# A mixture-of-experts stage with a fourth size class, its own PSUM banks for the down product, and weight loads half as large

## What is computed

```python
def expert(args):
    xe, e = args
    hu = xe @ w_up[e] + b_up[e]                       # (slots, 1024) @ (1024, 2048)
    gate = jnp.minimum(hu[:, :D_FF], SWIGLU_LIMIT)
    lin = jnp.clip(hu[:, D_FF:], -SWIGLU_LIMIT, SWIGLU_LIMIT)
    glu = gate * jax.nn.sigmoid(SWIGLU_ALPHA * gate)
    return ((lin + 1.0) * glu) @ w_down[e] + b_down[e]  # (slots, 1024) @ (1024, 1024)
```

## Time and profile before

| | before |
|---|---|
| median of the runs shown | 1485.96 us |
| span of the profiled execution | 1487.5 us |
| TensorE busy | 1238.6 us (83%) |
| VectorE busy | 402.2 us (27%) |
| ScalarE busy | 226.0 us (15%) |
| mean rate of the DMA over the span | 315 GB/s |
| mean granted TensorE clock | 0.934 of full speed |

### The profile page before, as it was taken

How to read it: one execution, slowest core, us unless ns; L and a number is a source line. 1 busy time by engine, 2 the same in 40 slices (tenths; PEclk the granted TensorE clock), 3 DMA queues, 4 the chain that set the end, 5 groups by cost and what they waited for, 6 DMA issues and landing times.

```text
span 1487.5 us, 21559 instructions
## 1 busy us (share of the span) xinstructions
PE 1238.6 (83%) x8297; PEld 615.4 (41%) x8306; DVE 402.2 (27%) x838; ACT 226.0 (15%) x376; POOL 94.1 (6%) x154
## 2 busy tenths in 40 slices
PE   3899898679649989989878998879967789897796
PEld 2554455545434444434324443434323333343243
DVE  0144113661471322112211211221212221232116
ACT  1211223001220110111111011110111111111111
POOL 0010002331330000000000000000000000000002
PEclk7799999888869999999999999999999999999998
DMA  9676537138214699899999789999899999999992
GB/s 311 243 217 188 179 113 214 49 114 244 113 57 173 270 418 382 338 382 417 419 418 418 315 338 385 417 418 419 330 418 416 419 419 419 415 418 419 418 416 109
DMA packets 116009, 467.94 MB, mean 315 GB/s; under 512 B 6978, under 2 KB 26118, under 8 KB 82953
## 3 DMA queue, kind: packets, MB, share of 16 engines
q1 hardware_dynamic: 100466, 455.61, 78.4%
q10 hardware_dynamic: 14966, 9.78, 2.2%
q0 software_dynamic: 544, 2.10, 0.6%
HBM read 461.31 MB, written 6.16 MB: 314 GB/s over the span
## 4 chain that ended last, share of the span: by engine, by line
PE 56%; DMA 33%; DVE 5%; ACT 2%; issue 2%; SPq 1%; POOL 0%; ACTq 0%; POOLq 0%; PEldq 0%; DVEq 0%
DMA mem<-in_w_up 31%; PE psum L780 19%; PE psum L811 8%; PE psum L513 6%; PE psum L822 3%; PE psum L757 3%; PE psum L498 3%; PE psum L697 2%; PE psum L517 1%; DMA mem<-in_w_mod 1%; PE psum L424 1%; PE psum L641 1%; ACT mem L1132 1%; PE psum L825 1%; DVE mem L1625 1%
## 5 line engine op out<-in xcount | busy, mean ns | idle before, releaser
L780 PE MATMUL psum<-mem 128*32 128x512 f32 (+2 forms) x2048 | 421.3, 630 | 126.8 <-DMA mem<-in_w_up 74.9
L780 PEld LDWEIGHTS psum<-mem 128*32 128x32 f32 (+2 forms) x2048 | 135.9, 133 | 406.8 <-issue 277.0
L811 PE MATMUL psum<-mem 128*32 128x512 f32 (+2 forms) x1024 | 204.8, 594 | 1.7 <-DMA mem<-in_w_down 1.7
L1718 DVE TENSOR_SCALAR mem<-psum 128x256 f32<-128x256 f32 (+2 forms) x32 | 20.0, 626 | 647.5 <-PE psum L785 647.5
L811 PEld LDWEIGHTS psum<-mem 128*32 128x32 f32 (+2 forms) x1024 | 102.9, 130 | 79.8 <-issue 50.6
L1737 DVE TENSOR_TENSOR mem<-mem,psum 128x1024 f32<-128x1024 f32 (+1 forms) x96 | 100.0, 1045 | 88.9 <-PE psum L822 71.2
L822 PE MATMUL psum<-mem 128*128 128x512 f32 x264 | 121.4, 602 | 1.2 <-ACT mem L1132 1.2
L1116 ACT ACTIVATE mem<-mem 128x256 f32<-128x256 f32 (+2 forms) x32 | 18.5, 579 | 483.3 <-DVE mem L1718 483.3
L757 PEld LDWEIGHTS psum<-mem 128*128 128x128 bf16 x2376 | 80.5, 99 | 21.4 <-issue 20.4
L513 PE MATMUL psum<-mem 128*128 128x512 f32 x192 | 86.3, 606 | 1.6 <-PE psum L424 1.6
L757 PE MATMUL psum<-mem 128*128 128x32 bf16 (+2 forms) x2376 | 83.9, 192 | 2.1 <-DVE mem L1694 2.1
(11 more groups left out here) (244 smaller groups left out, 918.5 us busy)
## 6 DMA issues: line engine op xcount, KB each, us to landing
mem<-in_w_up SPq DMA_DIRECT2D x128, 2048.0 KB, 23.5
mem<-in_w_down SPq DMA_DIRECT2D x64, 2048.0 KB, 19.7
mem<-in_w_mod SPq DMA_DIRECT2D x12, 2048.0 KB, 15.7
mem<-in_w_in SPq DMA_DIRECT2D x8, 2048.0 KB, 12.8
mem<-in_w_out SPq DMA_DIRECT2D x2, 2048.0 KB, 10.6
mem<-in_state_ret SPq DMA_DIRECT2D x4, 512.0 KB, 6.3
mem<-in_state_mlstm_c SPq DMA_DIRECT2D x4, 512.0 KB, 7.2
out_ret_s<-mem ACTq DMA_DIRECT2D x4, 512.0 KB, 3.2
```

The source lines that it names most:

```text
L780: last = pe.matmul(out, xg[:, 2 * c + j, 0:slots], moving, start=(c == 0 and j == 0), stop=False)
L811: last[c] = pe.matmul(psum[slots * q:slots * q + slots, 2 + u, :], actT[:, j, slots * q:slots * q + slots], at((4 + c) * SLOT, 4, D)[:, pi ...
```

## The change

1. A fourth size class of 96 slots. Experts with 65 to 96 tokens (0, 3 and 11) leave the class of 128. `up` for them does three groups of 32 slots (banks 0, 1, 2) times four quarters of the output columns, each matmul with 32 stationary columns in one column group: 96 matmuls of 512 columns, 192 records. `down` runs untiled with 96 stationary columns. The activations need 6 transposes in place of 8, their copy out is split in two by order, and VectorE's clips have 768 columns.
2. Twelve loads of 1 MB an expert, eight of w_up (one contraction piece each) and four of w_down, each with its own arrival and release semaphore. `down` waits for each w_down piece at its first use and gives each free at its last.
3. The down result goes to banks 6 and 7; the scatters go to banks 2 and 3, then 4 and 5, then 3; the placement transposes to bank 2. The wait for `y_copied` moves from ahead of `up` to ahead of the first scatter, where two waits for VectorE's clips are added (the scatter overwrites banks 2 and 3). The waits for `G_ready` and `added` move ahead of `up`.

```diff
-SIZES = (32, 64, 128)
+SIZES = (32, 64, 96, 128)
@@ by_size
+            with eng.If(count <= SIZES[1]):
+                with eng.If(count <= SIZES[0]):
+                    f(SIZES[0])
+                with eng.Else():
+                    f(SIZES[1])
+                eng.nop()
             with eng.Else():
-                with eng.If(count <= SIZES[1]):
-                    f(SIZES[1])
+                with eng.If(count <= SIZES[2]):
+                    f(SIZES[2])
                 with eng.Else():
-                    f(SIZES[2])
+                    f(SIZES[3])
+                eng.nop()
@@ SyncE
+            def expert_piece(e, c):
+                if c < UP:
+                    src = a["w_up"][0][e, 128 * c:128 * c + 128, :]
+                    dst = piece_slot(c, 2 * D)
                 else:
+                    src = a["w_down"][0][e, 256 * (c - UP):256 * (c - UP) + 256, :].rearrange("(j p) n -> p j n", p=128)
+                    dst = piece_slot(c, 2, D)
+                sp.dma_start(dst, src).then_inc(piece_in[c], 16)
             with sp.Fori(1, NE) as e:
-                for c in range(6):
-                    sp.wait_ge(used[c], e + USES[c])
-                    expert_chunk(e, c)
+                for c in range(PIECES):
+                    sp.wait_ge(piece_done[c], e)
+                    expert_piece(e, c)
@@ TensorE, up
-                if slots == 32:
+                if slots in (32, 96):
                     w = weights.rearrange("p (l n) -> p l n", l=2)
-                    return [(psum[32 * q:32 * q + 32, 0, :], w[:, :, 256 * q:256 * q + 256]) for q in range(4)]
+                    return [(psum[32 * q:32 * q + 32, g, :], slice(32 * g, 32 * g + 32), w[:, :, 256 * q:256 * q + 256])
+                            for g in range(slots // 32) for q in range(4)]
...
+                for c in range(UP):
+                    pe.wait_ge(piece_in[c], 16 * (it + 1))
+                    for out, cols, moving in up_products(slots, piece_slot(c, 2 * D)):
+                        last = pe.matmul(out, xg[:, c, cols], moving, start=(c == 0), stop=False)
+                    last.then_inc(piece_done[c], 1)
@@ TensorE, down
-                tiles = 128 // slots
+                tiles = 1 if slots == 96 else 128 // slots
...
-                for c in (4, 5):
-                    pe.wait_ge(loaded[c], 16 * (it + USES[c] + 1))
+                            if last[c] is None:
+                                pe.wait_ge(piece_in[UP + c], 16 * (it + 1))
...
-                last[0].then_inc(used[4], 1)
-                last[1].then_inc(used[5], 1)
+                for c in range(DOWN):
+                    last[c].then_inc(piece_done[UP + c], 1)
@@ TensorE, expert
                 pe.wait_ge(S("xg_ready"), ig + 1)
-                pe.wait_ge(S("y_copied"), it + 1)
+                pe.wait_ge(S("G_ready"), it + 1)
+                pe.wait_ge(S("added"), 3 * it + 1)
                 by_size(pe, count, lambda slots: up(it, slots))
                 gather(ig + 1, count_next)
-                pe.wait_ge(S("G_ready"), it + 1)
-                pe.wait_ge(S("added"), 3 * it + 1)
+                pe.wait_ge(S("y_copied"), it + 1)
+                pe.wait_ge(S("gate_ready"), it + 1)
+                pe.wait_ge(S("lin_clipped"), it + 1)
                 scatter(it, 0)
...
                 scatter(it, 2)
-                pe.wait_ge(S("added"), 3 * it + 3)
                 by_size(pe, count, lambda slots: down(it, slots))
@@ ScalarE, expert
+                    if slots == 96:
+                        by_piece = actT.rearrange("p j s -> p (j s)")[:, 0:n] \
+                            .rearrange("p (q h g s) -> p h g q s", q=4, h=2, g=3)
+                        by_turn = flat(0, n).rearrange("p (g h q s) -> p h g q s", g=3, h=2, q=4)
+                        act.copy(by_piece[:, 0], by_turn[:, 0])
+                        act.copy(by_piece[:, 1], by_turn[:, 1]).then_inc(S("actT_ready"), 1)
+                        return
...
-                act.copy(yd.rearrange("p u n -> p (u n)"), flat(2, D)).then_inc(S("y_copied"), 1)
+                act.copy(yd.rearrange("p u n -> p (u n)"), flat(6, D)).then_inc(S("y_copied"), 1)
```

More of the change, by code:

```diff
@@ L258, in build, with piece_slot @@
         used = [S(f"slot{c}_used") for c in range(6)]
+        UP, DOWN = 8, 4
+        PIECES = UP + DOWN
+        piece_in = [S(f"piece{c}_in") for c in range(PIECES)]
+        piece_done = [S(f"piece{c}_done") for c in range(PIECES)]
+        def piece_slot(c, *shape):
+            return at(c * SLOT // 2, *shape)
         def by_size(eng, count, f):
             if count is None:
-                f(SIZES[2])
+                f(SIZES[3])
                 return
-            with eng.If(count <= SIZES[0]):
-                f(SIZES[0])
+            with eng.If(count <= SIZES[1]):
[4 more added lines that the diff above has]
+                eng.nop()
             with eng.Else():
-                with eng.If(count <= SIZES[1]):
-                    f(SIZES[1])
+                with eng.If(count <= SIZES[2]):
+                    f(SIZES[2])
                 with eng.Else():
-                    f(SIZES[2])
+                    f(SIZES[3])
+                eng.nop()
         def flat(bank0, n):
@@ L390, in _ @@
                     with sp.Fori(0, NE) as e:
-                        for c in range(6):
-                            sp.wait_ge(used[c], r * NE + e + USES[c])
-                            expert_chunk(e, c)
+                        for c in range(PIECES):
+                            sp.wait_ge(piece_done[c], r * NE + e)
+                            expert_piece(e, c)
             with sp.Else():
@@ L763, in up_products @@
             def up_products(slots, weights):
[L766 removed]
+                if slots in (32, 96):
                     w = weights.rearrange("p (l n) -> p l n", l=2)
[L768 removed]
+                    return [(psum[32 * q:32 * q + 32, g, :], slice(32 * g, 32 * g + 32), w[:, :, 256 * q:256 * q + 256])
+                            for g in range(slots // 32) for q in range(4)]
                 if slots == 64:
[L770 removed]
+                    return [(psum[64 * q:64 * q + 64, lin, :], slice(0, 64),
+                             weights[:, D * lin + 512 * q:D * lin + 512 * q + 512])
                             for lin in range(2) for q in range(2)]
[L772 removed]
+                return [(psum[:, b, :], slice(0, 128), weights[:, 512 * b:512 * b + 512]) for b in range(4)]
             def up(it, slots):
[L775 to L782 removed]
+                for c in range(UP):
[3 more added lines that the diff above has]
+                    last.then_inc(piece_done[c], 1)
                 pe.wait_ge(S("bsel_ready"), it + 1)
[L784 to L785 removed]
+                for out, cols, moving in up_products(slots, bparts[:, 0:2 * D]):
+                    last = pe.matmul(out, bsel[:, cols], moving, start=False, stop=True)
                 last.then_inc(S("up_done"), 1)
@@ L809, in down @@
                             piece = q * pieces + j
[L810 to L813, removed]
+                            c = piece // 2
+                            if slots == 96:
+                                turned = actT.rearrange("p j s -> p (j s)")[:, 0:8 * slots] \
+                                    .rearrange("p (j s) -> p j s", j=KD)[:, piece, :]
+                            else:
+                                turned = actT[:, j, slots * q:slots * q + slots]
+                            if last[c] is None:
+                                pe.wait_ge(piece_in[UP + c], 16 * (it + 1))
+                            last[c] = pe.matmul(psum[slots * q:slots * q + slots, 6 + u, :], turned,
+                                                piece_slot(UP + c, 2, D)[:, piece % 2, 512 * u:512 * u + 512],
                                                 start=(j == 0 and q > 0), stop=(j == pieces - 1))
-                last[0].then_inc(used[4], 1)
-                last[1].then_inc(used[5], 1)
+                for c in range(DOWN):
+                    last[c].then_inc(piece_done[UP + c], 1)
             def scatter(it, t):
[L820 to L826, removed]
+                for u in range(2):
+                    out = psum[:, 2 + 2 * t + u, :] if t < 2 else psum[64 * u:64 * u + 64, 3, :]
+                    last = pe.matmul(out, G[:, tok(t)], yd[:, u, :], start=True, stop=True)
                 last.then_inc(S("scattered"), 1)
@@ L1128, in expert @@
                 act.wait_ge(S("scattered"), 3 * it + 3)
-                act.copy(G, psum[:, 7, 0:NTOK]).then_inc(S("G_ready"), 1)
-                act.wait_ge(used[4], it + 1)
-                act.wait_ge(used[5], it + 1)
-                act.copy(yd.rearrange("p u n -> p (u n)"), flat(2, D)).then_inc(S("y_copied"), 1)
+                act.copy(G, psum[:, 2, 0:NTOK]).then_inc(S("G_ready"), 1)
+                for c in range(UP, PIECES):
+                    act.wait_ge(piece_done[c], it + 1)
```

(7 more changed lines are left out.)

26 lines of the change are left out of this document (10 added, 16 removed).

## The result

The changed kernel takes 1949.56 us (four runs, 1946.22 to 1952.41) against 1485.39 us before (four runs, the three above and one of 1484.83): ratio 1.311, 95% interval 1.308 to 1.314. It is 31% slower, and nowhere near the 1440 us of the forecast.

The account below looks back on a forecast made before the run. Weight loads at 418 GB/s set the pace, with about 61 us of idle DMA around large experts. Gains 9.7 + 37.7 + 2.8 less 2.7 for boundaries make 47.5; 1487.5 - 47.5 = 1440.0 us, range 1431 to 1462.

Parts of the forecast that it names:

- The size class of 96: Large experts on TensorE: `up` 21.3 us in place of 29.4, 9.0 to `down`, `down` 13.75; sum 44.1 us.
- The banks: Between `down` and the next expert: the result's copy leaves the path, 1.64 us before, 0.2 taken for the branch.
- Rival 4: TensorE's loop: waits, deeper branches and the new arm's code add 3 us or more per expert; 1475 to 1490, chance 0.04.
- the walk: Large experts 0, 3, 11 and 17 followed in turn: gains of 9.7 and 37.7 us, 3 us idle left.
- The rival that 96 slots don't pack: Class-96 `up` stays 29.4 us, 8.1 longer three times, 21 us in all; time 1461, chance 0.11.
- Expert 0: Start of the loop: `up` ends at 475.0, `down` runs 484.0 to 497.7, expert 1's weights land earlier; gain 9.7 us.
- Behind expert 3: DMA after this large expert: w_down pieces come free before the queue needs them, idle 0 in place of 13.5 us.
- the 0.015 us: Cost taken for each of six added load boundaries per expert, 2.7 us over 30 experts.
- the 0.09 us of one window: Worst microsecond near a load boundary, 381 of 418; upper bound per added boundary, in a rival 16.6 us, time 1454, chance 0.14.
- Expert 30's last w_up piece: Sign near the end of the loop: it lands near 1371 us, before 1416.

Follow-up runs that it names:

- the kernel with the short loop: The changed kernel with the gather in two arms (64 and 128 slots) in place of four, all else kept: 1442.11 us, ratio 0.970.

## Why the prediction was wrong, point by point

**The step that failed** is the one that priced the new arm: "The size class of 96". It counted the 192 records that run and what they replace, and took the arm's code for free; the branch got 0.2 us under "The banks". The part that lies in no row of the trace before is the length of the code. It shows there only as an absence: 23 packets of the instruction queue, none in the loop. Rival 4 had the right kind of cause ("the new arm's code") with "3 us or more" an expert in it, a chance of 0.04 and a time of 1475 to 1490. The measured size is 16.4 us an expert: 1949.56 - 1442.11 = 507.5 over 31.

**What would have shown it beforehand.** The built program of before could be counted: 1,187 instructions in the loop, and 657 more by the change. No trace of before shows how many fit, so the 1,844 would have been a reason for a wide range and no more; a run of the kernel before with arms that nobody takes shows it without the change (1,743 fast, 1,791 slow).

**The rest of the walk mostly held**, as the kernel with the short loop shows, in which only the gather's arms differ from the change. Its chain (start, length, what):

```profile
451.18 20.81 PE psum L800 x192
...
498.50 7.05 PE psum L800 x64
...
523.88 1.06 PE psum L800 x8
...
538.98 20.81 PE psum L800 x192
...
568.82 13.73 PE psum L835 x32
582.55 13.88 PE psum L800 x64
...
1280.34 1.94 PE psum L800 x8
...
1340.58 1.87 PE psum L800 x8
```

- Class 96: `up` 20.81 us against 21.3 forecast, `down` 13.73 against 13.75; 538.98 to 582.55 is 43.6 against 44.1. The rival that 96 slots don't pack was wrong: 192 records took 0.108 us each, against 0.111 in class 32, so three groups of 32 keep all four column groups at work.
- Expert 0: expert 1 begins at 498.50 (497.9 forecast), but in part by luck. The stage began 0.9 us earlier. The forecast's end of `up`, 475.0 = 452.06 + 21.3 + 1.6, has 1.6 us for a low clock at its start (before, the first 2 MB took 9.0 us against 29.43 / 4 = 7.4 later, at a mean granted clock of 0.81). No run shows such a loss for 96 slots: here the granted clock was 1.00 from 451 to 461 us, and `up` took 20.81 us. What took that back is the way from the end of `up` (471.99) to `down` (484.76): 12.8 us in place of 9.0, with 1.9 us of "issue" inside the gather and slower scatters.
- Expert 2's last piece of w_up landed at 523.8, while 501.5 + 20.1 = 521.6 was forecast, so less of the idle time around expert 0 went than the 9.7 us. Expert 2 waited for that piece, where the forecast had it at TensorE's pace; so expert 3 begins at 538.98 (536.6 forecast). Expert 4 begins at 582.55, against 536.6 + 44.1 + 0.2 = 580.9.
- The banks: between the end of `down` (568.82 + 13.73 = 582.55) and the next `up` (582.55) nothing is left of 1.64 us.
- Idle time of the DMA, by windows of the same kernel:

```profile
454.50:501.00 46.50, 44.62 (x327) 17.28 (x323) 8.35 (x13) 4.25 (x7) 0.29 (x1) 0.96 0.67 255
501.00:590.00 89.00, 87.92 (x729) 36.14 (x723) 20.90 (x39) 13.83 (x20) 0.88 (x3) 1.00 1.02 418
590.00:650.00 60.00, 58.43 (x493) 24.99 (x490) 16.23 (x30) 9.66 (x14) 0.59 (x2) 1.00 1.02 418
...
830.00:920.00 90.00, 85.18 (x647) 34.59 (x644) 21.37 (x41) 13.56 (x20) 0.88 (x3) 0.97 1.00 409
920.00:1040.00 120.00, 111.84 (x758) 48.52 (x759) 27.54 (x51) 17.33 (x24) 1.18 (x4) 0.97 1.01 412
1040.00:1370.00 330.00, 285.16 (x2105) 106.80 (x2097) 72.97 (x143) 45.65 (x66) 3.23 (x11) 0.93 1.02 418
```

  Behind expert 3 nothing is idle (13.5 us before). Two windows below 418 are left, 90 x (1 - 409/418) = 1.9 and 120 x (1 - 412/418) = 1.7, together 3.6 against 3 forecast. The last window lies at 418 with twelve loads an expert, and two experts take 1340.58 - 1280.34 = 60.24 us, 30.12 each against 30.11 before. So no cost of a boundary shows: the 0.015 us (2.7 us in all) was not needed, and the 0.09 us of one window was no cost of a boundary.
- Expert 30's last w_up piece ended its wait at 1370.7, where about 1371 was forecast. That is luck in part: the start around expert 0 was 2.2 us worse, and the stretch behind it 2.2 us better, as the boundaries cost nothing.
- The release of w_down: the sections before the prediction say that both w_down slots come free only at the end of `down`. With 128 slots the first comes free halfway, as the prediction takes it and the earlier trace rows show (an issue from 497.99, in a `down` that ended at 504.7). With 32 slots all pieces come free at the end in both kernels.
- Sum: 1487.5 - 1439.4 = 48.1 us between the spans, against 47.5.
- The parts: without the class of 96 a gain of 29.6 us was measured against 1486.85 (20 expected); the class adds 15.2 to that, the smaller pieces 15.1. They don't add up to shares of their own, since each takes idle time that another would have taken.

So the forecast's own mechanism came to within 2 us once the loop was short, with two errors of 2.2 us that cancelled, and the answer was off by 510 us by a resource that it had not looked at.

## What to carry to other kernels

Before adding an arm to a branch in a loop, count the loop's instructions on the engine as built, dead arms included, and look at the instruction queue's packets inside the loop: none means that it fits, and that says nothing about how near it is to not fitting (here 25 packets in all at 1,743 instructions, 305 at 1,791). If idle time called "issue" appears at places without a wait, at changing spots of the same group of matmuls (here behind 53 and behind 35 of 72), look at that queue first. A branch arm that saves little (here the gather for 32 slots in place of 64, 0.3 us: 1.90 against 2.21 us before) can be dropped to pay for one that saves much.

## What was not expected of the hardware

- A loop of about 1,743 instructions on TensorE ran without fetches (25 packets of q8 in all), one of 1,791 with nine packets of 16.4 KB a round (305 in all); against 1488.18 us beside them that made 0.3% and 34% (1493.13 and 1993.23 us, one run each).
- The fetches cost 12.9 us a round with hardly any other traffic (1719.79 against 1318.66 us). What a fetch waits for is not settled: the transfer of a block and the time until it is asked for were not tried apart within the 1.4 us, part of which is work at a lower clock (mean granted 0.866 against 0.947).
- Whether the step depends on where the loop stands against the blocks stays open near the step (1,743 and 1,791 were run at one place each); at 1,631 instructions four placements made no difference beyond 5 us. Whether the step is set by how much code the engine keeps or by how far the loop jumps back was not tried: both grow with the loop.
